# Attention part in another order, products of zeros, a later end of the up/down pairs: one change to a four-layer fp32 kernel on one core

## The reference, cut to what matters

```python
def second_block(x, p, positions, ...):
    cos, sin = rope_tables_2(positions)
    h = x
    for i in range(DEPTH):                                    # DEPTH = 2
        a = rmsnorm_2(h, norm_mix_pre[i])
        u = jnp.einsum('bsd,de->bse', a, w_in[i])
        q, k, v, qi, ki, wi, u_conv, u_pool = jnp.split(u, IN_SPLITS_2, axis=-1)
        ...                                                   # q, k, qi, ki: partial_rope on 16 of 64 features
        y_attn = dsa_sparse_attention(q, k, v, qi, ki, wi)
        y_conv = conformer_conv(u_conv, ...)                  # a * sigmoid(g), 31 taps over time, layernorm, silu, product
        y_pool = multiscale_pool(u_pool, pool_w[i], pool_scale[i])
        mix = jnp.einsum('bse,ed->bsd', jnp.concatenate([y_attn, y_conv, y_pool], axis=-1), w_out[i])
        h = h + rmsnorm_2(mix, norm_mix_post[i])
        m = rmsnorm_2(h, norm_mlp_pre[i])
        m = jnp.square(jax.nn.relu(jnp.einsum('bsd,df->bsf', m, w_up[i])))      # 1024 -> 4096
        m = jnp.einsum('bsf,fd->bsd', m, w_down[i])
        h = h + rmsnorm_2(m, norm_mlp_post[i])
        gate = jax.nn.sigmoid(jnp.einsum('bsd,de->bse', h, ple_gate[i]))
        h = h + gate * jnp.einsum('bsp,pd->bsd', p[i], ple_proj[i])
    return h

def dsa_sparse_attention(q, k, v, qi, ki, wi):                # 8 heads, 2 of keys and values; 16 index heads
    ...
        dots = jnp.einsum('bthd,bsd->bths', qi_blk, ki_f)
        idx = jnp.einsum('bths,bth->bts', jax.nn.relu(dots), wi_blk) * idx_scale
        idx = jnp.where(causal[None], idx, -jnp.inf)
        _, sel = lax.top_k(idx, 64)
        ...                                                   # softmax over the 64 selected keys only
```

## Time and profile before

| what | value |
|---|---|
| time, median of 3 runs | 1998.05 us (1994.35 to 1999.39) |
| the profiled execution's own time | 1996.97 us |
| its span (first to last instruction) | 1995.1 us |
| mean granted clock of PE in it | 0.981 |
| PE busy | 1928.5 us, 97% |
| DVE busy | 1349.0 us, 68% |
| ACT busy | 996.9 us, 50% |
| POOL busy | 233.5 us, 12% |
| DMA engines, mean busy share over the span | 49.5% for the weights' queue |

### The profile page before, as it was taken

How to read it: one execution, slowest core, us unless ns; L and a number is a source line. 1 busy time by engine, 2 the same in 40 slices (tenths; PEclk the granted TensorE clock), 3 DMA queues, 4 the chain that set the end, 5 groups by cost and what they waited for, 6 DMA issues and landing times.

```text
span 1995.1 us, 36561 instructions
## 1 busy us (share of the span) xinstructions
PE 1928.5 (97%) x15864; PEld 1910.3 (96%) x15864; DVE 1349.0 (68%) x1609; ACT 996.9 (50%) x1231; POOL 233.5 (12%) x168
## 2 busy tenths in 40 slices
PE   7999999999999999999999999988999998889998
PEld 7999999999999999999999999987999998789998
DVE  6655777775559555787785558886856588675555
ACT  5433545564337434545563446766533476653333
POOL 3000100010002000100010002462100026610000
PEclk9999999999999999999999999989999999799999
DMA  8555554465554655544555555413455553236551
GB/s 266 184 183 181 157 172 160 134 205 190 190 196 149 211 191 191 171 130 156 166 174 200 183 183 160 148 48 127 156 202 171 175 155 107 69 123 213 172 195 60
DMA packets 246532, 329.56 MB, mean 165 GB/s; under 512 B 6246, under 2 KB 218788, under 8 KB 246372
## 3 DMA queue, kind: packets, MB, share of 16 engines
q1 hardware_dynamic: 246018, 326.79, 49.5%
q10 hardware_dynamic: 258, 0.16, 0.1%
q0 software_dynamic: 96, 0.26, 0.0%
HBM read 326.14 MB, written 1.05 MB: 164 GB/s over the span
## 4 chain that ended last, share of the span: by engine, by line
PE 79%; DVE 13%; ACT 4%; POOL 2%; issue 1%; DMA 1%; POOLq 0%; DVEq 0%; ACTq 0%; SPq 0%
PE work L2006 17%; PE work L2007 17%; PE work L2008 17%; PE acc L2006 8%; PE acc L2008 8%; PE acc L2007 8%; DVE w_lo L1300 4%; ACT w_hi L797 1%; POOL fa L744 1%; DVE ra L1313 1%; PE work L2133 1%; POOL fa L718 1%; DVE fa L1734 1%; DVE fa L1345 1%; PE acc L2076 1%
## 5 line engine op out<-in xcount | busy, mean ns | idle before, releaser
L2006 PE MATMUL work<-xh,w_hi 128*128 128x256 f32 x2560 | 723.6, 283 | 21.1 <-DVE w_lo L1300 10.3
L1300 DVE TENSOR_TENSOR w_lo<-raw,w_hi 128x2048 fp32r<-128x2048 f32 (+2 forms) x314 | 704.8, 2254 | 44.5 <-ACT w_hi L797 42.5
L2007 PE MATMUL work<-xl,w_hi 128*128 128x256 f32 x2560 | 720.7, 282 | 0.0
L2008 PE MATMUL work<-xh,w_lo 128*128 128x256 f32 x2560 | 719.2, 281 | 0.0
L797 ACT ACTIVATE w_hi<-raw 128x2048 fp32r<-128x2048 f32 (+2 forms) x314 | 578.3, 1850 | 170.1 <-PE work L2008 79.4
L2006 PEld LDWEIGHTS work<-xh,w_hi 128*128 128x128 f32 x2560 | 484.6, 189 | 24.9 <-issue 21.7
L2007 PEld LDWEIGHTS work<-xl,w_hi 128*128 128x128 f32 x2560 | 485.4, 190 | 0.3
L2008 PEld LDWEIGHTS work<-xh,w_lo 128*128 128x128 f32 x2560 | 485.2, 190 | 0.0
L1345 DVE TENSOR_TENSOR fa<-work,rstd 128x512 f32<-128x512 f32 x168 | 114.9, 689 | 397.7 <-PE work L2008 397.1
L2006 PE MATMUL acc<-ra,w_hi 128*128 128x256 f32 x1344 | 377.8, 281 | 0.0
L2008 PE MATMUL acc<-ra,w_lo 128*128 128x256 f32 x1344 | 377.4, 281 | 0.0
(11 more groups left out here) (289 smaller groups left out, 2301.0 us busy)
## 6 DMA issues: line engine op xcount, KB each, us to landing
raw<-in_ffn_w_gu_dram SPq DMA_DIRECT2D x88, 1024.0 KB, 5.1
raw<-in_w_in_dram SPq DMA_DIRECT2D x52, 1024.0 KB, 5.4
raw<-in_ffn_w_down_dram SPq DMA_DIRECT2D x44, 1024.0 KB, 5.1
raw<-in_w_up_dram SPq DMA_DIRECT2D x32, 1024.0 KB, 5.5
raw<-in_w_down_dram SPq DMA_DIRECT2D x32, 1024.0 KB, 6.9
raw<-in_w_mla_out_dram SPq DMA_DIRECT2D x8, 1024.0 KB, 5.0
raw<-in_w_o_dram SPq DMA_DIRECT2D x8, 1024.0 KB, 5.2
raw<-in_w_ple_gate_dram SPq DMA_DIRECT2D x8, 1024.0 KB, 5.4
```

The costliest lines, as they stand in the source:

```text
L1300: v.tensor_tensor(w_lo[:, s, 0:n], raw[:, r, 0:n], w_hi[:, s, 0:n].bitcast(F32), ALU.subtract).then_inc(lo_done.sem, 1)
L2006: pe.matmul(dst, ah, bh, start=start and i == 0, stop=False, skip_group_check=not group)
L2007: pe.matmul(dst, ah, bl, start=False, stop=False, skip_group_check=not group)
L2008: last = pe.matmul(dst, al, bh, start=False, stop=stop and i == len(pairs) - 1, skip_group_check=not group)
```

## The change

It has eight parts.

1. **Start.** The first chunk's first 1024 columns are copied by ACT and split by DVE before any row of the norm; the other half comes after one bank of rows (two rows). PE's first unit waits for the first half, and for the second at its fifth row.
2. **Rotation, split.** For index units 1 to 3 DVE rotates unit c before it splits a chunk that was split ahead of the rotation until now.
3. **Rows, taps.** ACT copies the second query unit's rows with no taps ahead. Two taps that stood ahead of the query part become one behind the rows; the two before the first exponential become three. DVE's rotation of the second query unit comes a round earlier, behind the key parts, and its query part too.
4. **Mask.** Instead of three passes there is one: (score - PICKED) - causal, over 384 columns; `masked_scores` then subtracts that where it added.
5. **Zero products.** `warm(dst, n)` issues n PE products of zero weights with 256 columns of a constant, into a part of PSUM that nothing reads: 16, 8, 14 and 6 in a layer's attention part, 36 ahead of the MLP's first products, 10 ahead of the gates.
6. **MLP entry.** The sum of squares is taken between the two halves of unit 2 rather than inside the pair.
7. **Up leads by three.** `down` of hidden part j - 3 follows `up` unit j; the chunk list and the splits follow.
8. **End.** The last gate unit is made as two products with a signal each. Sigmoid, product, sum and transposes run on halves.

```diff
@@ mlp_chunks, up_chunk, down_chunk
-    out = one(0) + one(1)
-    for j in range(2, steps):
-        out += one(j) + [(down, (j - 2) * 256, 2, 0, D)]
+    out = one(0) + one(1) + one(2)
+    for j in range(3, steps):
+        out += one(j) + [(down, (j - 3) * 256, 2, 0, D)]
...
@@ ACT, start of stage 1 (DVE's is its counterpart)
+            act.wait_ge(raw_full[0], 16)
+            act.activation(w_hi[:, 0, 0:CH // 2], raw[:, 0, 0:CH // 2], ACT.Copy).then_inc(first_hi, 1)
...
-                    norm_hi(here, 0, V1_FFN1, lambda b: (h_new, b - NB), squares=False, banks=range(2))
-                    split_hi(here, 0)
-                    norm_hi(here, 0, V1_FFN1, lambda b: (h_new, b - NB), squares=False, banks=range(2, NB))
+                    norm_hi(here, 0, V1_FFN1, lambda b: (h_new, b - NB), squares=False, banks=(0,))
+                    act.activation(w_hi[:, 0, CH // 2:], raw[:, 0, CH // 2:], ACT.Copy).then_inc(hi_done.sem, 1)
+                    norm_hi(here, 0, V1_FFN1, lambda b: (h_new, b - NB), squares=False, banks=range(1, NB))
@@ ACT, queries
-                some_taps(2)
                 hi_of_unit(here, U2["qt", 0], ("qt", 0), qh[:, 0:2, :], bank2(U2["qt", 0]))
                 rows_of(("q", 1), "q1", 1)
+                some_taps(1)
                 act.wait_ge(*pooled.at(here, 0))
                 act.activation(pyh, py, ACT.Copy).then_inc(part_hi.event(here, "pooly"), 1)
                 hi_of_unit(here, U2["qt", 1], ("qt", 1), qh[:, 2:4, :], bank2(U2["qt", 1]))
-                some_taps(2)
+                some_taps(3)
@@ ACT, MLP
-                    if j:
-                        next_hi(here, up_chunk(j))
+                    if j + 1 < MLP_STEPS:
+                        next_hi(here, up_chunk(j + 1))
@@ DVE, index queries
                 for c in range(1, 4):
                     rope_unit(("qi", c), c)
-                    if c == 1:
-                        next_lo(here, G2_IN)
+                    next_lo(here, QI2[c - 1] if c > 1 else G2_IN)
                     weighted(c - 1)
                     index_queries(c)
-                    next_lo(here, QI2[c])
+                next_lo(here, QI2[3])
@@ DVE, top-k rounds and mask
                     if r == 5:
                         keys_lo()
+                        rope_unit(("q", 1), "q1")
                     if r == 6:
-                        rope_unit(("q", 1), "q1")
-                    if r == 7:
                         queries_lo(0)
...
-                    last = v.tensor_scalar(work_b[:, a:a + n], work_a[:, a:a + n], PICKED, NEG, ALU.not_equal, ALU.mult)
...
-                chain(here, v.tensor_tensor(idx, work_b, causal, ALU.add))
+                chain(here, v.scalar_tensor_tensor(idx, work_a, PICKED, causal, ALU.subtract, ALU.subtract))
@@ DVE, MLP
-                    if j:
-                        next_lo(here, up_chunk(j))
+                    if 0 < j < MLP_STEPS - 1:
+                        next_lo(here, up_chunk(j + 1))
@@ DVE, end
+                def gated_half(a, ready_at):
+                    v.wait_ge(*ready_at)
+                    chain(here, v.tensor_tensor(gate[:, 3, a, :], gate[:, 3, a, :], pp2[:, 6 + a, :], ALU.mult))
+                    return v.tensor_tensor(h[:, 6 + a, :], h[:, 6 + a, :], gate[:, 3, a, :], ALU.add)
@@ PE
+            def warm(dst, n):
+                for _ in range(n):
+                    pe.matmul(dst, zero_r[:, :], rot_r[:, :, :].rearrange("p a b -> p (a b)"), start=True, stop=True,
+                              skip_group_check=True)
...
                 turned(("qt", 0), tm[:, 0, :, :])
+                pe.wait_ge(*dot_taken.at(here, 11))
+                warm(acc[:, 1, 0:T], 16)
                 pe.wait_ge(*unit_taken.at(here, U2["q", 1]))
                 turned(("qt", 1), tm[:, 1, :, :])
...
+                warm(acc[:, 1, 0:T], 8)
                 scores(0)
                 scores(1)
                 for hd in range(HEADS):
+                    if hd < 2:
+                        warm(acc[:, 1, 0:T], 14 - 8 * hd)
                     probs(hd)
...
-                pair(here, M2, (U2["up", 0], U2["up", 1]), normed(here, 1), "mlppre", 1, early=True)
-                for j in range(2, MLP_STEPS):
-                    project(here, up_chunk(j), U2["up", j])
...
-                    pe.wait_ge(hl_ready.sem, hl_ready.after(here, j - 2))
-                    accumulate(here, down_chunk(j - 2), hidden(j % 2), first=j == 2)
+                pair(here, M2, (U2["up", 0], U2["up", 1]), normed(here, 1), idle=36)
+                halves(here, up_chunk(2), U2["up", 2], lambda: summed(here, "mlppre", 1))
+                for j in range(3, MLP_STEPS + 2):
+                    if j < MLP_STEPS:
+                        project(here, up_chunk(j), U2["up", j])
...
+                    pe.wait_ge(hl_ready.sem, hl_ready.after(here, j - 3))
+                    accumulate(here, down_chunk(j - 3), hidden((j - 3) % 2), first=j == 3)
```

More of the change, by code:

```diff
@@ L116, in one @@
         return [(up, 0, KD, j * 256, 256)]
-    out = one(0) + one(1)
-    for j in range(2, steps):
-        out += one(j) + [(down, (j - 2) * 256, 2, 0, D)]
-    return out + [(down, (j - 2) * 256, 2, 0, D) for j in (steps, steps + 1)]
+    out = one(0) + one(1) + one(2)
+    for j in range(3, steps):
+        out += one(j) + [(down, (j - 3) * 256, 2, 0, D)]
+    return out + [(down, j * 256, 2, 0, D) for j in range(steps - 3, steps)]
 def chunks_1():
@@ L1267, in _ @@
                 next_layer(2)
-                gate_sigmoid(3)
+                if layer == DEPTH - 1:
+                    act.wait_ge(last_half, 1)
+                    act.activation(gate[:, 3, 0, :], acc[:, 1, 0:T], ACT.Sigmoid).then_inc(last_half, 1)
+                    act.wait_ge(unit_ready.sem, unit_ready.after(here, U2["gate", 3]))
+                    act.activation(gate[:, 3, 1, :], bank(U2["gate", 3])[:, 0:T], ACT.Sigmoid).then_inc(
+                        act_out.event(here, ("gate", 3)), 1)
+                else:
+                    gate_sigmoid(3)
                 next_layer(3)
@@ L1825, in _ @@
                     src, dst = dst, src
-                for tb in range(TB):
-                    a, n = P * tb, P * (tb + 1)
-                    last = v.tensor_scalar(work_b[:, a:a + n], work_a[:, a:a + n], PICKED, NEG, ALU.not_equal, ALU.mult)
-                chain(here, last)
-                chain(here, v.tensor_tensor(idx, work_b, causal, ALU.add))
+                chain(here, v.scalar_tensor_tensor(idx, work_a, PICKED, causal, ALU.subtract, ALU.subtract))
                 def rinv(hd):
@@ L2040, in halves, with pair @@
                 last.then_inc(unit_ready.sem, 1)
-            def pair(here, c, units, wait, name=None, norm=None, n=(2, 2), x=None, early=False):
+            def pair(here, c, units, wait, name=None, norm=None, n=(2, 2), x=None, idle=0):
                 x = x or (xh, xl)
@@ L2055, in pair @@
                             last.then_inc(unit_ready.sem, 1)
[L2056 removed]
+                    if k == KD - 1 and name is not None:
                         summed(here, name, norm)
@@ L2112, in ffn @@
                 if (f, here) == (F1, (1, 0)):
-                    pair(here, f, (u,), normed(here, n))
+                    free(here, u)
+                    pe.wait_ge(first_lo, 1)
+                    w = w_hi[:, 0, :], w_lo[:, 0, :]
+                    for k in range(KD):
+                        if k == KD // 2:
+                            weights(here, f)
+                        normed(here, n)(k)
+                        for m in range(2):
+                            done = product(bank2(u)[:, m, :], [(columns(w, k * 256 + m * P), tiles((xh, xl), everything, k, everything))],
+                                           start=k == 0 and m == 0, stop=k == KD - 1, group=False)
+                    done.then_inc(unit_ready.sem, 1)
                     project(here, f + 1, u + 1)
```

57 lines of the change are left out of this document (39 added, 18 removed).

## The result

| | median us | lowest to highest | n |
|---|---|---|---|
| before | 1997.76 | 1994.35 to 1999.39 | 4 |
| changed | 1984.97 | 1984.04 to 1985.57 | 4 |

What follows compares the result with a forecast made beforehand. PE, busy 97% of the span, was taken as the bound, with time only in its idle waits and low clock: 0.3 + 17.2 + 4.8 + 0.8 = 23.1 us off 1996.97, so 1974; range 1965 to 1985.

Steps and rivals of the forecast that it cites:

- What bounds the kernel, and the price of the clock: Whole kernel: PE is busy 97%; a product takes 212 ns at the low clock, 115 at full, 97 more.
- lead by three: MLP: up leading by three gives and costs nothing; the rival that it makes the kernel slower (2013) had chance 0.03.
- The start: Kernel's start: first product 3.5 us earlier, coming back as a wait of about 3 us for POOL; gain 0.3.
- Rotation, query rows, first exponential: Attention parts before the heads: first exponential, held by three taps, moves 3.0 us earlier in layer 0, 1.8 in layer 1.
- The mask: Attention part: one pass of 1.5 us replaces three; DVE gains 0.5, at most 1.4, PE nothing.
- The eight heads: Attention parts' heads: if zeros keep the clock up, DVE bounds; laid out 21.4 and 21.0 us, gains 5.4 and 7.0.
- a sign of being wrong: Attention parts: a low stretch running through the heads would show the forecast wrong.
- The rival that the clock falls anyway: Later heads' waits let the clock go, the loop keeps 2 us of its 12.4; 1983, chance 0.20.
- The part behind the heads: From the seventh transpose to the mean's product: POOL is then the later one; 2.2 and 0.8 us left to gain.
- The 3.0 us off for the clock: Both attention parts: 1.5 us a layer taken off because the clock will still fall here and there.
- Entry into the MLP: MLP's first products: 2.5 us from full clock, some 0.5 of wait, less 0.6 to 0.9 new wait; 2.4 a layer.
- The end: After the last sigmoid: DVE's 0.69 twice become halves of 0.4, ACT's sigmoid 0.6 to 0.4; gain 0.8 us.

Runs made afterwards that it cites:

- e5: The changed kernel with one of three taps left ahead of the first exponential, one behind it, one behind head 0's pooled rows; 1983.55 us, ratio 0.9927.
- e3: The changed kernel with ACT's output copy moved behind the tap and the chunk copy in the heads; 1983.18 us, ratio 0.9930.
- e9: The changed kernel with e3's ACT order and e5's taps, but the tap behind head 0's pooled rows put behind its output copy; 1976.89 us, ratio 0.9897.
- e2: The kernel before with only the attention part's zero products added (16, 8, 14 and 6 a layer); 1996.88 us, ratio 0.9999.
- e1: The changed kernel without any of its 180 zero products; 1987.24 us, ratio 0.9951.

## Why the prediction was right or wrong

- **What bounds the kernel, and the price of the clock**: right. 212 and 115 ns held, the MLP gave and took nothing, and lead by three cost nothing: the ledger stays at -5.87 through layer 0's MLP.
- **The start**: right in mechanism. The first product came at 12.81 (forecast: 3.5 us earlier, it was 3.6, 0.4 of it because the input landed earlier), and POOL took most of it back. But not as a wait of 3 us: it was 0.78, and the first 28 products ran at the low clock where 13 had. POOL's fold ended sooner than I allowed, its three adds took 6.95 us instead of 9.48, its last one 2.65 instead of 0.74. The stage gave 0.8 us instead of 0.3.

```profile
12.81 0.55 PE L2028 MATMUL work<-xh,w_hi 128*128 128x256 f32 x1 [3.40 <-DVE xl L1346]
...
18.07 6.95 POOL L721 TENSOR_TENSOR fa<-fa 128x512 f32<-128x512 f32 x3 [11.48 <-ACT fa L822]
25.09 2.65 POOL L725 TENSOR_TENSOR fa<-fa 128x256 f32<-128x256 f32 x1
...
27.80 0.70 PE L2097 MATMUL acc<-fa,consts 128*128 128x256 f32 x2 [0.78 <-POOL fa L725]
```

- **Rotation, query rows, first exponential**: right, 3.3 and 1.9 us for 3.0 and 1.8, the exponential held by three taps as laid out. e5 showed the price of those taps: 3.5 us at head 0 in layer 1.
- **The mask**: right that it moves nothing, wrong in size. I took 1.5 us for the pass, "since it stands in the same place with the same neighbour"; it took 0.56, in both layers.
- **The eight heads**: here the forecast failed, at the step "if they keep the clock up, DVE is the bound", from which 21.4 and 21.0 us followed. Neither half of it held. I added up DVE's rows and put PE's in the gaps, and left out ACT, whose page share of 50% looked idle. But ACT's queue is in order, and in it 1.91 us of chunk copy and 0.90 of tap stood behind a wait for PE and ahead of the next exponential. And the clock did not stay up: it was low for 10.2 us in each attention part, 6.8 of them in one stretch inside layer 0's heads, which the prediction had named as a sign of being wrong. The two hang together. Bringing ACT's work ahead of the wait (e3) took 4 us out of layer 0's heads, 3.4 of them by the clock that then stayed up there, and with the taps moved too (e9) they took 22.1 us, close to the layout. So for layer 0 the layout was that of a kernel with another order on ACT. For layer 1 it was not reached by any run (25.4 us in e9 against 21.0). The rival that the clock falls anyway was nearest in its number (1983), and right in that the clock fell among the later heads; but it took the clock for the only cause, and e2 raised it without a gain, while in e1 the part lost nothing without the zeros. Two readings of rows were off as well, neither of them the cause: 2.15 us for a chunk's split is the mean of three splits of 2048 columns (2.43) and one of 512 (1.32), so right only as a sum of the four; and the seventh head's transposes were read at 1732.57 in layer 1, but in layer 0 at 1358.25, where four transposes of the turned outputs stand ahead of them.
- **The part behind the heads**: 0.9 and -0.5 for 2.2 and 0.8. It starts later than laid out, with a wait of 1.8 and 1.7 us for the turned outputs (before: 1.7 and 1.1), which ACT copies behind a tap; in layer 1 the clock was low for 3.4 us behind that wait.
- **The 3.0 us off for the clock**: too little. 20.4 us of the two parts ran at the low clock with PE busy in nearly all of it, and at 212 ns a product instead of 115 that is, by my estimate, some 9 us of PE's time. Not all of it would be gained: a faster PE meets the waits above.
- **Entry into the MLP**: 1.9 and 2.0 for 2.4. The terms held one by one: the zeros fitted inside the wait (the first product came at 1392.16, 4.39 us after the end of the last sum, where the wait had been 4.48), and the new wait for chunk 2 was 0.69, of the 0.6 to 0.9 forecast. e1 shows that the zeros themselves brought 0.85, the rest of the edit (the moved sum above all) the other 1.1: without zeros the slow products hide that same wait for DVE.

```profile
1391.08 1.00 PE L2037 MATMUL work<-rot_r,zero_r 128*128 128x256 f32 x7
1392.16 0.39 PE L2028 MATMUL work<-xh,w_hi 128*128 128x256 f32 x1
...
1404.91 0.36 PE L2028 MATMUL work<-xh,w_hi 128*128 128x256 f32 x1 [0.69 <-DVE w_lo L1312]
```

- **The end**: right, 0.9 for 0.8 (DVE's two steps 0.42 each for 0.69).

Left open: how much of e3's gain is the chunk copy and how much the tap (they were moved together), what holds layer 1's heads above the layout, and the worth of zeros in layer 1, where POOL's chain covers it.

## What to carry to other kernels

Where a loop passes through several engines, lay out each engine's queue in order, the half idle ones too: what stands in a queue behind a wait and ahead of what others wait for is on the path, whatever that engine's share of busy time. A fast clock is worth something only where PE isn't waiting already: look for what it will meet. The other way round, a short wait can cost more than its length: here one of 0.75 us went together with 3.4 us of slower products. So test the order and the clock together, not only each by itself. And when PE is faster, ask which slow chain (POOL's taps here) then ends last, before moving work about.

## What was not expected of the hardware

The mask's pass reads two SBUF tensors beside POOL, as the pass before did, which took 1.51 us. The new one took 0.56, and the add that POOL began 0.01 us after it took 1.70 instead of the 1.28 of its neighbours. DVE's and POOL's rows of layer 1:

```profile
1690.36 0.56 DVE L1842 SCALAR_TENSOR_TENSOR fa<-fa,consts 128x384 f32<-128x384 f32 x1
...
1690.37 1.70 POOL L747 TENSOR_TENSOR fa<-fa 128x512 f32<-128x512 f32 x1
```

So which of the two pays depends on which began first; that is what the Trainium skill says in "SBUF — State Buffer", Who interferes with whom (issue order, not the shape, decides who blocks), and both traces agree. I had taken the long time for a property of the place. In the old kernel the pass began at 1700.00, 0.3 us into one of POOL's adds (1699.68, two in 2.97 us), and ended 0.4 us after that add.
